# Expert gates of a routed layer: scattered into a table in memory by adding transfers, instead of spread by one-hot products

## The reference, cut to what matters

```python
q = (xf @ wq).reshape(t, PEER_HEADS, PEER_QDIM)
s1 = einsum('thd,kd->thk', q[..., :half], keys1); s2 = einsum('thd,kd->thk', q[..., half:], keys2)
v1, i1 = lax.top_k(s1, PEER_TOPK); v2, i2 = lax.top_k(s2, PEER_TOPK)
cand_s = v1[..., :, None] + v2[..., None, :]
cand_i = i1[..., :, None] * PEER_KEYS + i2[..., None, :]
top_s, pos = lax.top_k(cand_s, PEER_TOPK)            # 16 of 256 pairs of keys
expert = take_along_axis(cand_i, pos, axis=-1)
gate = softmax(top_s)
z = einsum('cd,ced->ce', xc, u[ec])                  # dot of token and expert row
act = gelu(z) * gc
out = einsum('ce,ced->cd', act, v[ec])
```

## Time and profile before

| | us |
|---|---|
| median of 3 runs (lowest, highest) | 3149.4 (3147.65, 3151.55) |
| the profiled execution, its own time | 3157.57 |
| the profiled execution, first to last instruction (span) | 3155.8 |
| U0 / U1 / V0 | 177.1 / 172.5 / 162.6 |
| U2 / V1 / U3 | 172.9 / 162.0 / 173.8 |
| V2 / V3 | 182.8 / 167.2 |

### The profile page before, as it was taken

One profiled execution on the slowest core, in us unless ns is written; L12 is line 12 of the kernel. 1 busy time (PEld: TensorE's weight loads), 2 busy tenths in 40 slices (PEclk: granted clock), 3 DMA queues, 4 the chain that ended last, 5 costly groups with the idle time before them and its releaser, 6 DMA issues.

```text
span 3155.8 us, 62000 instructions
## 1 busy us (share of the span) xinstructions
PE 3110.9 (99%) x24718; PEld 3005.3 (95%) x24718; DVE 2421.7 (77%) x3900; ACT 1744.5 (55%) x2400; POOL 325.3 (10%) x311
## 2 busy tenths in 40 slices
PE   8999999999999999999999999999999999999998
PEld 8999999999999999999999988999999999999997
DVE  8767776755556776666668998987799789988886
ACT  6444545677776656555654545555455545554444
POOL 4000000000000000000000012331133112310110
PEclk9999999999999999999999999999999999999999
DMA  5444435444444555454455555678867787665785
GB/s 189 158 162 146 167 117 209 161 160 161 168 163 173 176 177 183 174 181 175 163 190 187 183 201 201 244 262 287 288 242 249 281 282 248 244 208 185 266 283 188
DMA packets 117821, 637.38 MB, mean 202 GB/s; under 512 B 11632, under 2 KB 32496, under 8 KB 50416
## 3 DMA queue, kind: packets, MB, share of 16 engines
q1 hardware_dynamic: 98496, 565.49, 51.1%
q0 software_dynamic: 18864, 68.43, 6.5%
q10 hardware_dynamic: 288, 1.05, 0.1%
HBM read 632.57 MB, written 2.36 MB: 201 GB/s over the span
## 4 chain that ended last, share of the span: by engine, by line
PE 76%; DVE 16%; DVEq 3%; DMA 2%; ACT 1%; issue 1%; POOL 0%; ACTq 0%; POOLq 0%; SPq 0%
PE bank L675 14%; PE bank L677 14%; PE bank L676 14%; PE bank L1211 9%; DVE wl L1863 6%; PE bank L1158 4%; PE bank L1212 4%; PE bank L1159 2%; PE bank L1201 2%; PE bank L1203 2%; PE bank L1202 2%; DVE hot_a L2543 1%; DMA raw<-peer_v 1%; DVEq L2562 1%; PE bank L829 1%
## 5 line engine op out<-in xcount | busy, mean ns | idle before, releaser
L1863 DVE TENSOR_TENSOR wl<-raw,wh 128x1024 fp32r<-128x1024 f32 x1052 | 1269.3, 1240 | 349.6 <-ACT wh L1349 340.2
L1349 ACT ACTIVATE wh<-raw 128x1024 fp32r<-128x1024 f32 x1052 | 1052.4, 1050 | 384.2 <-DMA raw<-w_in_a 124.5
L676 PE MATMUL bank<-hhl,wh 128*128 128x256 f32 x3568 | 991.4, 278 | 0.0
L675 PE MATMUL bank<-hhl,wh 128*128 128x256 f32 x3440 | 967.7, 281 | 0.8 <-DVE hhl L1911 0.8
L677 PE MATMUL bank<-hhl,wl 128*128 128x256 f32 x3440 | 954.2, 277 | 0.0
L676 PEld LDWEIGHTS bank<-hhl,wh 128*128 128x128 f32 x3568 | 675.3, 189 | 1.9 <-issue 1.7
L675 PEld LDWEIGHTS bank<-hhl,wh 128*128 128x128 f32 x3440 | 648.0, 188 | 4.7 <-issue 2.0
L677 PEld LDWEIGHTS bank<-hhl,wl 128*128 128x128 f32 x3440 | 646.8, 188 | 0.0
L1158 PE MATMUL bank<-hhl,wh 128*128 128x448 f32 x1920 | 624.1, 381 | 9.2 <-DVE wl L1863 8.0
L1159 PE MATMUL bank<-hhl,wl 128*128 128x224 f32 x2048 | 521.7, 265 | 0.0
L1211 PE MATMUL bank<-ahl,wh 128*128 128x448 f32 x1488 | 474.2, 375 | 3.2 <-DVE ahl L2569 3.1
(11 more groups left out here) (461 smaller groups left out, 4435.6 us busy)
## 6 DMA issues: line engine op xcount, KB each, us to landing
raw<-peer_u SPq DMA_DIRECT2D x128, 1024.0 KB
raw<-peer_v SPq DMA_DIRECT2D x128, 1024.0 KB
raw<-w_in_c SPq DMA_DIRECT2D x64, 1024.0 KB
raw<-w_in_a SPq DMA_DIRECT2D x63, 1024.0 KB
raw<-w_kv SPq DMA_DIRECT2D x32, 1024.0 KB
raw<-w_in_b SPq DMA_DIRECT2D x32, 1024.0 KB
raw<-w_out_a SPq DMA_DIRECT2D x16, 1024.0 KB
raw<-w_out_b SPq DMA_DIRECT2D x16, 1024.0 KB
```

Of the source, the lines that this page charges most:

```text
L675: eng.matmul(out, h_[:, k, :], high[:, k, :], start=(k == 0), stop=False)
L676: eng.matmul(out, h_[:, k, :], low[:, k, :], start=False, stop=False)
L1349: eng.activation(high_half(c, half), raw_half(c, half), ACT.Copy).then_inc(hi_ready, 1)
L1863: eng.tensor_tensor(low_half_out(c, half), raw_half(c, half), high_half(c, half).bitcast(F32), ALU.subtract).then_inc(lo_ready, 1)
```

## The change

The spread products are gone. Instead a table of 16384 x 224 gates lies in memory (`gate_cells`, 14.7 MB).

1. During the pair loop of stage F (long before the routing) SP's queue writes zeros into it: 8 transfers of 1.8 MB in pieces of 512 bytes (`zero_gates`).
2. After each head, VectorE forms the gates and the table addresses of that head in small operations on 32 elements, hung between the low halves of the next head (`gates_of_head`); ScalarE does an Exp per head (`gate_exps_after`).
3. GpSimd issues for each head 32 indexed transfers of up to 128 single values with an add in memory (`scatter_gates`), and waits before the next head until all of them have landed. Heads can choose the same expert for a token, the slots of one head can't.
4. After the eighth head, GpSimd starts reading the table back, in 64 pieces of 128 partitions x 448 values, into four buffers (`gates_in`); VectorE multiplies each piece into the activations in one operation per two units (`gate`). The pieces for block 0 are used at the last three units of U1 and the first 13 of V0, the others at every second unit of U2, U3 and V2.
5. The halves of z are no longer copied to `z_parts`: ScalarE copies the low half (224 wide, `z_low`), VectorE adds it to the bank (`add_dots`, also between the halves of the routing). The bank is one of four now instead of two.
6. `paired_v_block` is gone; V2 uses `v_block` like the others. The fetching of rows moves out of U1 and V3 into V0 to V2, and the lower row sums from V2 to U3.
7. ScalarE's first high part of activations for V0 comes after the last gelu of U1 (it stood ahead of it).

The core of the diff:

```diff
+            def zero_gates(i):
+                n = P * DENSE // PAIRS
+                eng.dma_start(gate_table[:, ds(i * n, n)].rearrange("a (g z) -> a g z", z=P),
+                              zeros.unsqueeze(1).broadcast_to([P, n // P, P])).then_inc(sQ["zeroed"], 16)
...
-                eng.tensor_tensor(z, z_parts[:, n % 2, 0:DENSE], z_parts[:, n % 2, DENSE:2 * DENSE], ALU.add).then_inc(sQ["z_step"], 1)
+            def scatter_gates(h):
+                eng.wait_ge(sQ["routed"], h + 1)
+                if h > 0:
+                    eng.wait_ge(sQ["scattered"], 16 * NT * PEER_TOPK * h)
+                for k in range(PEER_TOPK):
+                    for t in range(NT):
+                        n = min(P, DENSE - t * P)
+                        eng.indirect_dma_start(
+                            out=gate_cells, out_offset=bass.IndirectOffsetOnAxis(ap=cell[0:n, t, h * PEER_TOPK + k:h * PEER_TOPK + k + 1], axis=0),
+                            in_=tops[0:n, t, h, k:k + 1], in_offset=None, compute_op=ALU.add).then_inc(sQ["scattered"], 16)
+            def gates_in(g):
+                b, c = g // (BJ // 2), g % (BJ // 2)
+                if g >= GATE_PARTS:
+                    eng.wait_ge(sQ["gated"], g - GATE_PARTS + 1)
+                eng.dma_start(gates[g % GATE_PARTS][:, :, :].rearrange("p e t -> p (e t)"),
+                              gate_table[:, (b * BJ + 2 * c) * DENSE:(b * BJ + 2 * c + 2) * DENSE]).then_inc(gate_in[g % GATE_PARTS], 16)
...
-                        if b >= 1 and not (isinstance(i, int) and i * PER_PAIR + c >= TURNS):
-                            spread(b - 1, i, c)
...
-                    eng.activation(z_parts[:, c % 2, :], B[DOT_BANK[b] + c % 2][:, 0:2 * DENSE], ACT.Copy).then_inc(s["z_step"], 1)
+                    eng.activation(z_low[:, :], B[DOT_BANK[b] + c % DOT_BANKS][:, DENSE:2 * DENSE], ACT.Copy).then_inc(s["z_step"], 1)
...
                     eng.activation(z, z, ACT.Gelu).then_inc(s["z_read"], 1)
+                    if b == 1 and isinstance(i, int) and i > 0 and c == PER_PAIR - 1:
+                        act_high(0, 0, 0)
...
+            def gate(name, n):
+                if (name, n) in GATE_AT:
+                    eng.wait_ge(gate_in[g % GATE_PARTS], 16 * (g // GATE_PARTS + 1))
+                    eng.tensor_tensor(part, gates[g % GATE_PARTS][:, :, :], part, ALU.mult).then_inc(s["gated"], 1)
+            def add_dots(b, n):
+                eng.wait_ge(s["z_step"], 2 * (b * BJ + n) + 1)
+                eng.tensor_tensor(acts[b % 2][:, n, :], bank[:, 0:DENSE], z_low[:, :], ALU.add).then_inc(s["z_step"], 1)
...
+                    if b == BLOCKS - 2 and n == BJ - 1:
+                        act_low(b + 1, 0, 0)
```

More of the change, by code:

```diff
@@ L72 @@
         ROW_AT[_k, _n] = len(ROW_AT)
-X_ROWS_AT = 9
-ROWS_DOTTED_AT = 5
-ROWS_GATED_AT = 8
-LOWER_ROWS_SUM_AT = 2
-G_SCALE = 2.0 ** 14
+assert len(ROW_AT) == 4 * ROWS
+ROWS_DOTTED_AT = 8
+ROWS_GATED_AT = 11
+LOWER_ROWS_SUM_AT = 24
+GATE_PARTS = 4
+GATE_AT = {}
+for _s, _n in ([("U1", n) for n in range(BJ - 3, BJ)] + [("V0", n) for n in range(BJ // 2 - 3)]
+               + [(_k, 2 * n + 1) for _k in ("U2", "U3", "V2") for n in range(BJ // 2)]):
+    GATE_AT[_s, _n] = len(GATE_AT)
 FH = KC // 2
@@ L1193, in u_block @@
                 body(BJ // PER_PAIR - 1)
-            def value_products(bank, k, c, j, n, opens, closes):
-                for e in range(2):
-                    w_h, w_l = wh[k % RAW][:, j * FH + 2 * n + e, :], low_rows(k, j * FH + 2 * n + e)
-                    out_ = bank[:, e * T:e * T + DENSE]
-                    a_h, a_l = ah[c % 2][:, j, :], al[c % 2][:, j, :]
-                    eng.matmul(out_, w_h, a_h, start=opens and e == 0, stop=False)
-                    eng.matmul(out_, w_h, a_l, start=False, stop=False)
-                    last = eng.matmul(out_, w_l, a_h, start=False, stop=closes and e == 1)
-                return last
             def wide_products(bank, k, c, j, m, first, final):
@@ L1330, in _ @@
             u_block(3)
-            paired_v_block(2)
+            v_block(2)
             v_block(3)
@@ L1841, in _ @@
             for name, b in PEER_ORDER:
-                if name == "U":
+                if name == "U" and b == 0:
+                    for i in range(BJ // PER_PAIR):
+                        gelus(b, i)
+                elif name == "U":
                     gelus(b, 0)
@@ L2462, in top16 @@
                     eng.match_replace(scratch[n], vals[n][:, 0:8], src[n], TAKEN)
-                low()
+                low(*steps[1:2])
                 eng.drain()
@@ L2466, in top16 @@
                     eng.max(vals[n][:, 8:16], scratch[n])
-                low()
+                low(*steps[2:3])
                 eng.drain()
@@ L2475, in route, with low @@
                 halves_of_head = iter(range(ROUTE_HALVES * h, ROUTE_HALVES * (h + 1)))
-                def low():
+                after = [lambda: None] * 4 if h == 0 else gates_of_head(h - 1)
+                def low(n=None):
+                    if n is not None:
+                        after[n]()
                     n = next(halves_of_head)
-                    low_half(0, ROUTE_FIRST + n // 2, n % 2)
+                    low_half_and_dots(ROUTE_FIRST + n // 2, n % 2)
                 eng.wait_ge(s["sc_ready"], h + 1)
                 top16([vtop[:, n, :] for n in range(4)], [itop[:, n, :] for n in range(4)],
-                      [S12[:, n // 2, h, (n % 2) * P:(n % 2 + 1) * P] for n in range(4)], [w[:, :] for w in rest], low)
+                      [S12[:, n // 2, h, (n % 2) * P:(n % 2 + 1) * P] for n in range(4)], [w[:, :] for w in rest], low, (0, 1, 2))
                 k4 = [P, 4, PEER_TOPK, PEER_TOPK]
@@ L2567, in act_low, with low_half_and_dots @@
+            def low_half_and_dots(c, half):
+                low_half(0, c, half)
+                if half == 1 and c >= BASE["U0"] + 2:
+                    add_dots(0, c - BASE["U0"] - 2)
             def act_low(b, f, c):
@@ L2653, in gate_turns @@
                     low_half(0, u, 0)
[L2654 to L2655 removed]
+                    gate(f"U{b}", n)
                     low_half(0, u, 1)
[L2657 removed]
+                    add_dots(b, n)
+                    if b == BLOCKS - 1 and n == LOWER_ROWS_SUM_AT + 1:
+                        add_rows(0, 7)
+                    take_row(f"U{b}", n)
             def add_experts(b, f, first=0, end=None):
```

411 lines of the change are left out of this document (148 added, 263 removed).

## The result

The changed kernel takes **3300.52 us** (median of 4 runs, 3292.94 to 3308.08) and the kernel before 3148.53 (4 runs, 3145.17 to 3151.55): a ratio of 1.0475 with a 95% interval of 1.046 to 1.049, 4.7% slower. The profiled execution took 3302.37 us, of which the span is 3300.3. The forecast was 3134 with a range of 3114 to 3212, so the sign was wrong and the time lies far outside.

The account below looks back on a forecast made before the run. TensorE was taken to bound U1 to V2, VectorE the routing from about 1840 to 1917. -49.6 + 23 + 3.7 + 6.3 + 2 = -15, with the chain just in time, took 3149.4 to 3134 us (range 3114 to 3212).

Parts of the forecast that it names:

- t: GpSimd's time from issue to issue of a scatter: forecast 1.34 us, on time up to 1.35, break-even at 1.41.
- the chain: GpSimd's scatters from about 1741, 32 t + w per head, then the first table read; forecast just in time.
- What leaves TensorE: Spreads gone from U1, U2, U3 and V2 (10.1 us each), and V2's triples made pairs (9.2): -49.6 us.
- U0, +23: U0 grows by 23 us (6 to 31): 10.8 for small operations and adds on VectorE, 12 for contention with GpSimd.
- the lock: In U0, VectorE and GpSimd exclude each other from shared SBUF ports; scatters replacing adds lengthen VectorE's path by 12 us.
- (a) start of V0: TensorE waits at V0 because ScalarE makes the first high part only after U1's last gelu: +3.7 us.
- (b) start of V3: TensorE waits at V3 because the first low part stands behind V2's eight bank sums on VectorE: +6.3 us.
- Zeros, +2: Zeroing the table, 8 x 1.8 MB ahead of weights on SP's queue: 0 to 20 us, taken as +2.
- The sum without the chain, -15: Total of the terms for TensorE, U0, V0, V3 and the zeros, with no stall from GpSimd's scatters: -15 us.
- w: GpSimd's wait per head for its last scatter to land: forecast 3.5 us.
- rival (2): Scatters much slower, from adds in memory and shared transfer engines: at 2.1 us each 3326 us; chance 0.13 with all beyond.
- The deadline, 2125: Time when the table's first piece is due at U1's unit 29 on VectorE, counted back from V0's start: 2125.

Follow-up runs that it names:

- e1: Changed kernel with GpSimd's transfer of x issued after the scatters of head 1, not head 4: 3297.41 us.
- e6: Changed kernel with scatters that write instead of add, and the transfer of x after head 1: 3159.83 us.
- e2_half: Changed kernel that scatters only the first 8 of the 16 slots of each head, 128 transfers instead of 256: 3124.99 us.
- e7: e2_half with TensorE's short gaps at V0, V3, U2 and V2 taken away by reordering VectorE, ScalarE and row operations: 3109.80 us.
- e5: Changed kernel with scatters that write instead of add, the transfer of x still after head 4: 3187.22 us.
- e4: Changed kernel without any scatter, plus probes on GpSimd in stage A (plain transfers, indexed adds, writes, reads, eight of each): 3148.37 us, one run.
- e9: Changed kernel, gaps closed, x early, block 0 gated by spreads, table for blocks 1 to 3, head 0 writing, last 64 scatters over V0 and U2: 3134.36 us.
- e11: e9 with no row operation in the turn of U2 where x_half is loaded again; head 0's scatters still writes: 3128.81 us.

## Why the prediction was wrong, step by step

Two steps failed, and each of them turns the sign, the second by the estimate at the end of this section. The issue of a scatter was built up from a fetch, so that the add in memory stood in t at nothing: it costs 0.54 us per issue, and with x early it alone makes 3297 us of 3160 (e1, e6). And the sum counted one reader behind the chain where there are two: VectorE also waits for the copy of x. The steps in the order of the prediction:

- **What leaves TensorE, -49.6: right in kind, with gaps beside it that it didn't see.** U1 takes 162.5 us in e2_half (1942.3 to 2104.8, where the wait at V0 begins), as forecast. U2 and V1 take 331.05 us by VectorE's first adds of U2 and U3 (lines below), where the kernel before has 334.9: 3.9 less and not 10.1, since a gap of 3.5 us lies in U2, where x_half is loaded again, with low clock behind it. V0 takes 166.3 from its first product, where it took 162.6. U3 and V2 take 330.5 (U3 begins at 2606.1, 6.4 us ahead of its first add, V2 ends where the gap of V3 begins) and not 356.6: 26.1 less of the 29.4 put down, with a gap of 2.5 in V2. The prediction had a sign for this, a U2 of over 165 us with VectorE as the bound. The length came, 168.4 us in e2_half and 170.3 in the changed kernel, but VectorE was busy in only 131 and 132 us of it: the cause is a few waits for single operations and not a full VectorE. The gaps were on no list of the prediction; e7 gives 15 us back with them and the two below closed.

```profile
1765.64 0.39 DVE L2497 TENSOR_TENSOR act<-bank,z_low 128x224 f32<-128x224 f32 x1 [0.92 <-ACT z_low L1732]
...
1948.00 0.39 DVE L2497 TENSOR_TENSOR act_odd<-bank,z_low 128x224 f32<-128x224 f32 x1 [0.39 <-ACT z_low L1732]
...
2281.45 0.38 DVE L2497 TENSOR_TENSOR act<-bank,z_low 128x224 f32<-128x224 f32 x1
...
2612.50 0.39 DVE L2497 TENSOR_TENSOR act_odd<-bank,z_low 128x224 f32<-128x224 f32 x1
```
```profile
2943.42 0.74 PE L1193 MATMUL bank<-ahl,wh 128*128 128x448 f32 x1 [6.88 <-DVE ahl L2507]
```

- **U0, +23: wrong, +5.3.** From the first add of U0 to that of U1 are 182.4 us in e2_half, against a stage of 177.1. The 10.8 of small operations and adds fit it: less the 5 named below they make 5.8. The 12 for the lock are not there: it is one-sided. VectorE's 1216 ns beside the scatters and without them say that it doesn't wait for them; the 1304 beside GpSimd's adds went with the adds, 58 x 0.09 = 5 us back. The failed step is "the two engines keeping each other off SBUF", carried from an add, which reads two operands of 224, to an issue of a transfer. The Trainium skill (SBUF — State Buffer, "SBUF: two separate sides") lets whichever starts first, a VectorE operation with two SBUF inputs or a GpSimd operation that reads SBUF, block the other. Here the adds and VectorE agree with that; for the scatters only one half shows, GpSimd's (1.49 us with VectorE still, 1.86 beside low halves), and the measurement decides.
- **(a) start of V0, +3.7 and (b) start of V3, +6.3: right.** 3.80 and 6.97 us in the changed kernel, 3.9 and 6.9 in e2_half. Not in the sum was the low clock behind them, about 3 us at V3.
- **Zeros, +2: nothing.** On the queue of weights stage F takes 409.6 us from its first load of w_kv to the first of w_out_b, and took 411.6.
- **The sum without the chain, -15: near in size, and in part by luck.** The two long gaps taken out, -18; e2_half -24. Two errors stood against each other in it, 18 too much in U0 and the gaps not seen.
- **The chain, its form: right.** It began at 1735.0 (forecast 1741), w was 3.0 us on average (21.0 in 7 times; 3.5), and later heads never bound it. What came is rival (2), scatters that are much slower, with the wait for x ahead of the one at line 2491; its reason, that the weights use the same transfer engines, isn't what the runs show, since the price stands at GpSimd's issue. At t = 2.1 it gave 3326; t was 1.96 and the time 3300.5. It was given 0.13 together with all beyond.
- **The chain, t = 1.34: wrong, and this made most of the loss.** A scatter was built up from the fetch, 0.94 + 0.25 + a gap of 0 to 0.30. For a write this is nearly right: 0.97 + 0.30, and 0.25 to 0.29 more beside VectorE, 1.43 on average. But the gap is 0.30 nearly always, not the middle, and the add has a price of its own at the issue, 0.54 us on average and 138 us in all (e1 against e6), which no row of the trace of before showed. The text said so of the add "in memory", and then took the middle of a range that left it out. In the routing t was 2.05, next to the far bound of 2.1.
- **The deadline, 2125: wrong, about 2100.** VectorE comes to the gate at 2092 or 2093 (e2, e6), and its lead covers 8 us more (a wait of 40.4 for 32.1 on TensorE in e6). 18 of the 25 are the U0 that did not lengthen, the rest is U0's start, 7 to 8 us earlier in these runs than in the profile of before. A stage that grows less than feared moves the deadline forward: the errors of two steps were not independent.
- **A deadline that was missed altogether.** The copy of x went from GpSimd's turn 9 of U0 to a place behind 160 scatters, and VectorE waits for it (line 2512) before it makes up the row numbers near the end of U0. "4 us for the transfers of x in between" counted what they cost GpSimd, not who waits for them. Even at t = 1.35 the fifth head would have been out at 1735 + 5 x 46.7 = 1968, 40 us after VectorE wanted it. In the changed kernel this is the longest wait, and in e1 it is shown to cost nothing further there; in e5 against e6 it costs 27 us. So the sign would have been wrong even with the forecast t: a wait of 40 us on VectorE is some 36 on TensorE (58.3 for 54.8 in e5), and the 3125 us of e2_half with it are about 3161, 12 above the kernel before. That is an estimate; no run had this t.

## What to carry to other kernels

When a chain of transfers on one queue gets a deadline, write down every instruction that now stands behind it on that queue with its own reader, and the time at which each is wanted; the last one is not the only deadline. A price that no row shows belongs in the range with both its ends, and if the sign hangs on it, the forecast should not sit on the cheaper side. And when a long wait is found, ask what waits next before counting it as a gain: here 132 us were removed for 3.

## What the runs showed of the hardware that was not expected

- An indexed transfer of 128 single values costs GpSimd 0.97 us to issue as a write, 0.94 as a read and 1.55 as an add (the shortest of eight each, e4), with a gap of 0.30 before each in a row of them; for adds 96 rows cost 1.43 and 32 rows 1.33.
- Low halves on VectorE, with both operands in SBUF, stretch an add's issue from 1.49 to 1.86 us on average (single ones to 2.69), and a VectorE that adds a bank in PSUM to a tile doesn't (1.49). VectorE isn't slowed by them: its low halves take 1.22 us either way, but 1.47 beside an add that GpSimd computes itself.
- Adds of single values beside the weights show no cost to TensorE but their chain: 3125 us with 128 of them, 3132.5 with none, and 3131 with 256 once their waits are taken out. The kernel without any ran at a lower granted clock; what lowered it isn't known.
- In three kernels TensorE waited on issue for some us beside writes of single values, and in the probes beside reads as well (10 us there, 4 to 5 in e9 and e11). Other kernels with such writes didn't show it.
